# Prompt attention of a hybrid decoder step, in 12 units of a head pair instead of 24 of a head pair and a row tile

## What is computed

```python
def masked_softmax(logits, mask):
    logits = jnp.where(mask, logits.astype(jnp.float32), NEG_INF)
    m = jnp.max(logits, axis=-1, keepdims=True)
    e = jnp.where(mask, jnp.exp(logits - m), 0.0)
    return e / jnp.maximum(jnp.sum(e, axis=-1, keepdims=True), TINY)
...
    logits = (jnp.einsum('btgrd,bsgd->bgrts', qg, k).astype(jnp.float32) * ATTN_SCALE
              - alibi_slopes()[None, :, :, None, None] * dist.astype(jnp.float32))
    pr = masked_softmax(logits, mask)
    o = jnp.einsum('bgrts,bsgd->btgrd', pr.astype(v.dtype), v)
...
    logits = jnp.concatenate(
        [jnp.einsum('bthd,bshd->bhts', q, k).astype(jnp.float32) * ATTN_SCALE
         + cq_t - jnp.swapaxes(ck, 1, 2)[:, :, None, :] for k, _, _, ck in segs], axis=-1)
...
    o_a = ng[..., 0:1] * o_cmp + ng[..., 1:2] * o_sel + ng[..., 2:3] * o_win
```

## Time and profile before

| | us |
|---|---|
| median of 3 executions | 924.46 (921.75 to 925.11) |
| profiled execution | 927.73 |
| its span in the trace | 926.0 |
| PE busy | 858.2 (93%) |
| DVE busy | 513.4 (55%) |
| ACT busy | 378.6 (41%) |
| POOL busy | 161.3 (17%) |
| DMA | 191.89 MB, mean 207 GB/s |

### The profile page before, as it was taken

The page is one execution under the profiler, slowest core; times in us unless marked ns, Lnnn a source line. Parts: engine busy times, 40 slices in busy tenths (PEclk is TensorE's granted clock), DMA queues, the critical chain, the costliest instruction groups (busy, mean ns, idle before and its releaser), DMA issues. The chain is left out here.

```text
span 926.0 us, 17951 instructions
## 1 busy us (share of the span) xinstructions
PE 858.2 (93%) x7159; PEld 703.4 (76%) x7159; DVE 513.4 (55%) x941; ACT 378.6 (41%) x704; POOL 161.3 (17%) x262
## 2 busy tenths in 40 slices
PE   4999878799999999999998977999979999999997
PEld 3788768689989977655754455997678998989985
DVE  5466567533434566754467434655656565565654
ACT  4346575633334324453224322444243443444432
POOL 2000041311121022333434510000001010110100
PEclk8999989999999899999999999999979999999999
DMA  6442096155424259999999995974054544555412
GB/s 219 150 160 105 10 316 236 60 145 134 165 107 184 92 229 398 346 333 416 406 417 420 388 404 169 297 250 164 10 196 142 162 137 136 177 195 171 136 45 61
DMA packets 90640, 191.89 MB, mean 207 GB/s; under 512 B 7466, under 2 KB 68682, under 8 KB 78186
## 3 DMA queue, kind: packets, MB, share of 16 engines
q0 software_dynamic: 15408, 106.04, 29.4%
q1 hardware_dynamic: 74876, 83.91, 29.0%
q10 hardware_dynamic: 288, 0.97, 0.3%
HBM read 187.44 MB, written 7.64 MB: 211 GB/s over the span
## 5 line engine op out<-in xcount | busy, mean ns | idle before, releaser
L1627 PEld LDWEIGHTS banks<-consts_base,stream_rows 128*128 128x128 f32 x672 | 73.2, 141 | 33.9 <-issue 26.8
L1875 ACT ACTIVATE keys_turned<-banks 128x512 f32<-128x512 f32 x94 | 55.0, 597 | 98.4 <-PE banks L1627 96.2
L258 PE MATMUL banks<-tokens_turned_high,w_gates_high 128*128 128x288 f32 x288 | 86.6, 301 | 3.3 <-PEq L191 2.3
L1627 PE MATMUL banks<-consts_base,stream_rows 128*128 128x128 f32 x672 | 82.7, 276 | 7.4 <-DVE fox_probs_turned L1866 2.6
L259 PE MATMUL banks<-tokens_turned_low,w_gates_high 128*128 128x288 f32 x288 | 85.5, 297 | 0.0
L1166 PE MATMUL banks<-chunks_turned_high,cmp_w_high 64*128 64x256 f32 (+1 forms) x512 | 78.6, 300 | 5.3 <-DVE cmp_w_low L251 2.7
L260 PE MATMUL banks<-tokens_turned_high,w_gates_low 128*128 128x288 f32 x272 | 81.8, 301 | 0.0
L1166 PE MATMUL banks<-chunks_turned_low,cmp_w_high 64*128 64x256 f32 (+1 forms) x512 | 75.4, 287 | 0.0
L1166 PE MATMUL banks<-chunks_turned_high,cmp_w_low 64*128 64x256 f32 (+1 forms) x512 | 75.1, 286 | 0.0
L1856 DVE COPY keys_turned<-banks 128x512 f32<-128x512 f32 x74 | 50.2, 689 | 32.7 <-PE banks L1627 30.2
L251 DVE TENSOR_TENSOR chunks_turned_low<-banks,chunks_turned_high 128x512 fp32r<-128x512 f32 x64 | 41.1, 683 | 46.9 <-ACT chunks_turned_high L246 46.9
(11 more groups left out here) (451 smaller groups left out, 2099.1 us busy)
## 6 DMA issues: line engine op xcount, KB each, us to landing
w_up_gate<-in_w_up SPq DMA_DIRECT2D x12, 1024.0 KB, 7.3
w_up_gate<-in_w_gate SPq DMA_DIRECT2D x12, 1024.0 KB, 9.8
w_down<-in_w_down SPq DMA_DIRECT2D x12, 1024.0 KB, 4.9
w_in_slot<-in_w_in SPq DMA_DIRECT2D x7, 1424.0 KB, 6.0
w_gates<-in_w_in SPq DMA_DIRECT2D x10, 512.0 KB, 6.8
cmp_w<-in_cmp_w_k SPq DMA_DIRECT2D x4, 512.0 KB
cmp_w<-in_cmp_w_v SPq DMA_DIRECT2D x4, 512.0 KB
stream_rows<-in_state_win_k SPq DMA_DIRECT2D x8, 256.0 KB
```

The source lines that it names most:

```text
L258: nc.tensor.matmul(out, lh, rh, start=start, stop=False, **kw)
L1627: ins = nc.tensor.transpose(bank(t)[:, q * P:(q + 1) * P], src, ident)
L1875: copy = lambda a, b: nc.scalar.activation(a, b, ACT.Copy)
```

## The change

- **Units.** 12 units: (sel, r) and (win, r) for r = 0..3 in turn, then (fox, r). An NSA unit has heads r and r+4 (one of each kv head), a fox unit heads 2r and 2r+1; both row tiles are in the unit.
- **Logits.** `c.qp`, `c.fqp` keep 4 slots, head j of the pair on partitions 64j to 64j+63 without zeros; each logit matmul contracts 64 partitions, on one of the two row halves, into a PSUM bank of its own.
- **DVE** takes each of the 4 logit tiles with one `tensor_tensor_reduce` (add of a bias table, and the minimum of the negated sum): a new constant table `pbias` for NSA; for fox POOL writes mask plus running sum into a tile and over that table.
- **Scaling before turning.** Shares of all 4 row groups at once; then probabilities are multiplied by them: tile 0 by DVE, tile 1 by POOL (NSA) or DVE (fox).
- **Turned probabilities** leave PSUM by DVE (tile 0) and ACT (tile 1).
- **Values** are the stationary operand, 64 columns, turned probabilities stream (128 columns), the two heads on the two column halves. Sel and win add up in one PSUM pair. The sums come out transposed, in `c.oap`, `c.obp`; so decode's 16 transposes go, and its `branch` steps are two splits.
- **POOL's list** is rewritten: its 8 normalisations stand between the gathers, the sums over `past_logf` stay last.
- **Compressed branch.** 8 logit matmuls of 2 x 16 columns (copy `kd` of the keys by group) instead of 16 of 16; values by 4 matmuls of 256 columns instead of 2 of 512, transposed sums.

```diff
--- before.py
+++ after.py
...
-    "prompt": ("pdist", "pmask"),
+    "prompt": ("pmask",),
+    "alibi": ("pbias",),
...
-            nc.gpsimd.memset(c.qp[:, :, :], 0.0)
-            nc.gpsimd.memset(c.fqp[:, :, :], 0.0)
...
-                        dst = (c.qp[rows, g * NR:(g + 1) * NR] if q == 0 else c.fqp[rows, g:NH:2])[:, :, t * P:(t + 1) * P]
+                        dst = (c.qp if q == 0 else c.fqp)[rows, :, t * P:(t + 1) * P]
...
-    units = [(br, t, pair) for br in ("sel", "win", "fox") for t in range(QT) for pair in range(NH // 2)]
-    U = len(units)
+    units = [(br, r) for r in range(NR) for br in ("sel", "win")] + [("fox", r) for r in range(NR)]
+    U, N = len(units), 2 * NR
+    part = lambda t: slice(0, P) if t == 0 else slice(P, P + SEQ)
+    T_LAG, PV_LAG = 2, 3
...
+            def past_sums(half):
+                by_pair = lambda x: x.rearrange("p b (j h) -> p b j h", h=2)
+                by_row = lambda x: x.rearrange("p (j b h) -> p b j h", j=4, h=2)
+                lf, after = past_logf[:, half * 4:half * 4 + 4], c.logf_after[:, half]
+                pool.wait_ge(past_logf_in, 16 * DB)
...
+            def normalise(m):
+                pool.wait_ge(share_ready, m + 1)
+                x = s[m % 3][:, :, part(1)]
+                nc.gpsimd.tensor_tensor(x, x, bcast(den[m % 3][:, 1, :], 2, SEQ), ALU.mult).then_inc(normed[1], 1)
...
+            for m in range(N):
+                normalise(m)
+                if m < 2:
+                    chunks.gather(2 + m)
+                if m == 2:
+                    pool.wait_ge(logf_ready, 1)
+                    keep(*pieces[-1])
+                if 3 <= m < 7:
+                    for b in range(2):
+                        past_rows(2 * (m - 3) + b)
+                if m == 4:
+                    fox_bias_first()
+                if m >= 5:
+                    fox_bias_second(m - 5)
+            fox_bias_second(NR - 1)
...
+            def scores(m):
+                br, r = units[m]
+                if m >= 2:
+                    pe.wait_ge(neg, 4 * (m - 1))
+                for t in range(QT):
                     for j in range(2):
...
+                        rows = slice(j * HD, (j + 1) * HD)
+                        q, k = (c.fqp, c.fkT[rows, r, 0:t + 1, :]) if br == "fox" else (c.qp, c.kT[rows, 0 if br == "sel" else 1, 0:t + 1, :])
+                        ins = nc.tensor.matmul(logits(m, t, j), q[rows, r, t * P:(t + 1) * P], k, start=True, stop=br != "fox", skip_group_check=True)
+                    for j in range(2):
+                        for kt in range(t + 1 if br == "fox" else 0):
+                            ins = nc.tensor.matmul(logits(m, t, j)[:, kt * P:], nlf[:, kt, 2 * r + j:2 * r + j + 1].to_broadcast([P, P]),
+                                                   up[:, 0:(t + 1 - kt) * P], start=False, stop=(kt == t), skip_group_check=True)
+                ins.then_inc(qk, 1)
...
+            def turn(m):
+                for t in range(QT):
+                    if t and units[m][0] == "fox":
+                        pe.wait_ge(fox_normed, m - N + 1)
+                    else:
+                        pe.wait_ge(normed[t], m + 1)
+                    if m:
+                        pe.wait_ge(copied[t], m)
                     for j in range(2):
                         for kt in range(t + 1):
...
+                            at = (j * (t + 1) + kt) * P
+                            ins = nc.tensor.transpose(c.ps[3 - t][:, at:at + P], s[m % 3][:, j, (t + kt) * P:(t + kt + 1) * P], c.k("ident"))
+                    ins.then_inc(turned[t], 1)
...
+            def values(m):
+                br, r = units[m]
+                if br == "sel" and r:
+                    pe.wait_ge(nsa_out, r)
+                if br == "fox":
+                    pe.wait_ge(nsa_out, NR)
+                    if r:
+                        pe.wait_ge(fox_out, r)
+                for t in range(QT):
+                    pe.wait_ge(copied[t], m + 1)
+                    for kt in range(t + 1):
+                        for j in range(2):
+                            off = {"sel": O_SV, "win": O_WV, "fox": O_FV + r * P}[br] + j * HD
+                            ins = nc.tensor.matmul(both[j * HD:(j + 1) * HD, t, r, :], z[:, kt, off:off + HD], pT[m % 2][:, j, t + kt, :],
+                                                   start=(br != "win" and kt == 0), stop=(br != "sel" and kt == t), skip_group_check=True)
+                ins.then_inc(pv, 1)
...
+            def exponentials(m):
+                for t in range(QT):
+                    for j in range(2):
+                        act.wait_ge(neg, 4 * m + 2 * t + j + 1)
+                        x = s[m % 3][:, j, part(t)]
+                        nc.scalar.activation(x, x, ACT.Exp, scale=-1.0, bias=nm[m % 3][:, t, j:j + 1], accum_out=den[m % 3][:, t, j:j + 1]).then_inc(probs, 1)
...
+            def take_logits(m):
+                br, r = units[m]
+                dve.wait_ge(qk, m + 1)
+                if m >= 3:
+                    dve.wait_ge(turned[0], m - 2)
+                    dve.wait_ge(turned[1], m - 2)
+                if br == "fox":
+                    dve.wait_ge(fox_bias, 2 + r)
+                for t in range(QT):
+                    for j in range(2):
+                        nc.vector.tensor_tensor_reduce(s[m % 3][:, j, part(t)], logits(m, t, j), bias_of(m, t, j), -1.0, FAR, ALU.add, ALU.min,
+                                                       nm[m % 3][:, t, j:j + 1]).then_inc(neg, 1)
...
+            def normalise(m):
+                dve.wait_ge(share_ready, m + 1)
+                for t in range(QT if units[m][0] == "fox" else 1):
+                    x = s[m % 3][:, :, part(t)]
+                    nc.vector.tensor_tensor(x, x, bcast(den[m % 3][:, t, :], 2, (t + 1) * P), ALU.mult).then_inc(fox_normed if t else normed[0], 1)
...
+            for n in range(U + T_LAG):
+                if n < U:
+                    take_logits(n)
+                if n == 0:
+                    forget_logs()
+                if n == 1:
                     dve.wait_ge(cum_ready, 1)
...
+                    nc.vector.tensor_copy(cq[:, :, :], c.ps[3][:, 0:2 * NH].rearrange("p (t h) -> p t h", t=QT)).then_inc(cum_out, 1)
+                if n >= T_LAG:
+                    take_turned(n - T_LAG)
+                if 1 <= n <= U:
+                    shares(n - 1)
+                    normalise(n - 1)
+                if 4 <= n < 4 + N and n % 2 == 0:
+                    nsa_rows_out((n - 4) // 2)
...
-                    pe.wait_ge(kc_done, 1)
+                    pe.wait_ge(kd_ready, 2)
                     pe.wait_ge(vh_ready, 2)
                     for t in range(QT):
-                        for h in range(NH):
-                            ins = nc.tensor.matmul(c.ps[7][:, (t * NH + h) * PCH:(t * NH + h + 1) * PCH], c.qp[:, h, t * P:(t + 1) * P],
-                                                   c.kcT[:, ND:ND + PCH], start=True, stop=True)
+                        by_head = c.ps[7][:, t * NH * PCH:(t + 1) * NH * PCH].rearrange("p (g r c) -> p g r c", g=NG, r=NR)
+                        for r in range(NR):
+                            ins = nc.tensor.matmul(by_head[:, :, r, :], c.qp[:, r, t * P:(t + 1) * P], kd[:, :, :], start=True, stop=True)
...
-                    nc.tensor.matmul(c.ps[7][:, :] if t == 0 else bank(NSTEP - 2, 0)[:, :], pcT[:, t, :], vh[:, :], start=True, stop=True).then_inc(ppv, 1)
+                    for j in range(2):
+                        ins = nc.tensor.matmul((c.ps[7] if t == 0 else bank(NSTEP - 2, 0))[:, j * SEQ:(j + 1) * SEQ], vh[:, (2 * t + j) * P:(2 * t + j + 1) * P],
+                                               pcT[:, :, :].rearrange("p t n -> p (t n)"), start=True, stop=True)
...
-            def turn_branch(step):
-                i, t = step[3], first[step]
-                free_bank(t)
-                for j in range(4):
-                    ins = nc.tensor.transpose(bank(t)[:, j * P:(j + 1) * P], (c.oa, c.ob)[i // 2][:, i % 2, j * P:(j + 1) * P], ident)
                 ins.then_inc(turned, 1)
 
...
-                    split_high(nc, o_cols(c.branch_high, i), o_bank(t)).then_inc(branch_high, 1)
+                    split_high(nc, o_cols(c.branch_high, i), (c.oap, c.obp)[i][:, :, :]).then_inc(branch_high, 1)
...
+                if kind == "branch":
+                    dve.wait_ge(branch_high, i + 1)
+                    split_low(nc, o_cols(c.branch_low, i), (c.oap, c.obp)[i][:, :, :], o_cols(c.branch_high, i))
```

305 lines of the change are left out of this document (127 added, 178 removed).

## The result

| | before | after |
|---|---|---|
| median of 9 runs, us | 925.11 (921.32 to 929.25) | 919.19 (915.55 to 923.1) |
| ratio, 95% interval | | 0.9937 (0.9914 to 0.996) |
| profiled execution, us (span) | 927.73 (926.0) | 920.28 (918.4) |

The kernel became 5.9 us (0.6%) faster. The forecast was 11.4 faster. The profiled pair differs by 7.45 us, and the trace splits that well. I use five marks: the start of compression (SP's first load of it), its first and its last output matmuls, the start of the FFN, and the end. The prompt stage itself starts at 113.1 in both.

What follows compares the result with a forecast made beforehand. No engine filled the prompt stage (waits in each unit's round bound it), and DMA bound decode. Prompt stage -7.5, compression -4.6 and its start +0.7 gave -11.4 us, so 924.5 became 913.1 us, range 905 to 922.

Steps and rivals of the forecast that it cites:

- The walk to the end of computing: Prompt stage: unit-by-unit timing from ACT's first exponential at 117.45 us to the end of computing at 170.2.
- POOL's stretch: Prompt stage, products 3 to 7: POOL's products, gathers and bias tiles take 17.9 us against 13.6 on DVE, pacing four units.
- I leave that at 159.6: Prompt stage's end: small gathers still land at 159.6, POOL's sums last 10.9 us to 170.5, next stage starts at 171.5.
- Start of compression: First part of compression: PE stands idle longer before it, costing +0.7 us (0 to +2).
- Compression's logits: Compression: 32 narrow records become 16, 2.3 us instead of 4.66, and PE's clock stays full: -4.6 us (-2.4 if it falls).
- Decode and what follows it: Decode: 16 transposes and two PSUM rounds go, but DMA sets the pace: 0 us (-1.9 to +1).
- POOL and DVE block each other: Rival, prompt stage: DVE's product over 256 and POOL's over 512 wait for each other, +4.8 us, 917.9; chance 0.18.
- The gathers land later: Rival, prompt stage: last small gather issued 7 us later, landing follows issue, POOL ends 5 later, 918 us; chance 0.12.
- The halves don't share: Rival, PE's half-array matmuls: +1.4 us in each of six units and the tail, only compression gains, 920.5 us; chance 0.07.
- Everything better: Rival, prompt stage: rows land earlier, fox units near 3.6 us, next stage at 166 to 167, 908 us; chance 0.12.
- The clock drops in the prompt stage: Rival: PE at half clock from 131 on, next stage at 194.7, total 935.6 us; chance 0.06.
- The changes of shape: PE: switching from 64-row to 128-row tiles costs 0.09 us each, three per NSA unit, six per fox unit.

Runs made afterwards that it cites:

- the bias on ScalarE: On the kernel with early gathers, POOL's 1.91 us first-tile fox bias operation replaced by eight small ones on ScalarE in units 3 to 6: 910.92 us, ratio 0.9866.
- early gathers: Changed kernel with POOL's eight past_logf gathers issued sooner (two before the first unit, two each in units 2 to 4): 913.36 us, ratio 0.9896.
- the bias earlier on POOL: On the kernel with early gathers, POOL's first-tile fox bias operation moved from unit 4 to unit 2: 917.32 us, ratio 0.993.
- head after head: Changed kernel with a pair's matmuls reordered, all of head 0 before head 1 (its results are wrong): 918.74 us, ratio 0.9947.
- the last kernel above: Changed kernel plus early gathers, fox bias on ScalarE, both tiles' logits before the forget sums, and window-state copies behind the stores, not waited for: 907.22 us, ratio 0.9807.
- all products on DVE: On the kernel with early gathers, the second tile's probabilities in the eight gated units weighted on VectorE instead of POOL: 914.84 us, ratio 0.9896.
- the sums grouped: On the kernel with early gathers, both tiles' logits ahead of all forget sums of a fox unit: 913.18 us, ratio 0.9887; with the bias on ScalarE too, 912.12, 0.9868.
- the copies behind the stores: Changed kernel with only the two window-state copies moved last in SP's prompt-stage queue and waited for at the kernel's end: 916.8 us, ratio 0.9878.

## Why the prediction was half right

**The walk to the end of computing: 170.2 forecast, 170.7 measured with ACT's last copy (PE's end is 170.3), and that is no confirmation.** The kernels with the same units and the gathers or copies elsewhere ended PE's computing at 167.3 to 167.7, the one with the bias on ScalarE at 164.5. The forecast lacked a hole and a clock: product 5 came late behind POOL's bias tile, PE stood idle 2.6 us and then ran at half clock for 10. I had priced POOL's stretch (17.9 us from product 3 to 7; 129.3 to 150.1 measured, 20.8) and not asked what PE's clock does in it. POOL's own work was 18.0 of the 20.8; for the other 2.8 it waited, ahead of product 7, for DVE's shares, which waited for PE: POOL did not pace the whole stretch. What made up for it was ahead of that stretch, where product 3 began at 129.3 and not 131.3, and mainly DVE, which I had at 41.5 us and which was busy for 35.8. Its instructions took about what I had put in, but in a row they overlap. DVE in order of time:

```profile
124.88 0.42 DVE L997 CUSTOM_DVE_ANT_0 prompt_logits<-banks,consts_alibi 128x256 f32<-128x256 f32 x1
125.22 0.08 DVE L997 DVE_READ_ACCUMULATOR2_ANT prompt_negmax<- 128x1 f32 x1
125.22 0.42 DVE L1022 COPY prompt_probs_turned<-banks 128x256 f32<-128x256 f32 x1
125.56 0.16 DVE L1004 TENSOR_SCALAR prompt_sums<-prompt_sums 128x4 f32<-128x4 f32 x1
```

The next one starts 0.34 us after one of 0.42. I had overlap in PE's prices, taken from the starts of neighbours, and left it out of DVE's.

**The step that failed: "I leave that at 159.6", and 10.9 and 1.0 us behind it.** The floor was named and its three terms were all too small. The rows landed 1.6 us later; the sums took 11.8, since the first half (fifteen in 5.42 us and one of 0.58, against 4.93 and 0.25 before) ran beside DVE's last units; and behind POOL the next stage took 2.0 us to start, not 1.0. Together 3.5, and 171.5 + 3.5 is the 175.0 measured. The reason given, that the same bytes go through the same queues, was half of the truth: the landing depends on both. Issued 9.6 us sooner the rows landed 9.3 sooner (151.9); issued at about the same time without the copies in the stage, at least 9.8 sooner.

**Start of compression: 0.7 forecast (0 to 2.0), 2.1 measured.** The price is at the upper end of the bound: PE was idle from 170.3 to 175 and at half clock to 187. With the idle time down to 1.2 us (early gathers) the price is 0. But its size does not follow the idle time alone: with 4.2 us idle (the bias earlier on POOL) and with 8.1 (head after head) it was 0.8, and 0.8 again in the last kernel above, with 1.2.

**Compression's logits: 4.6 forecast, 4.9 measured**, 3.3 when undone by itself. The mechanism is shown, the size is known only to lie near these two.

**Decode and what follows it: 0 forecast, 0.7 measured.** The 16 transposes less moved nothing that can be told from the 588 to 591 us which the rest of the program took in the kernels here. Projection: 0 forecast, 0 measured (the prompt stage starts at 113.1 in both).

**The rivals.** *POOL and DVE block each other*: yes, though not at the price or the place given. In the pairs that the rival named, DVE's product over 256 began first and took 0.42 to 0.43 us, as in the units where it ran alone, and POOL's took 1.23 to 1.28 in five units against 1.05 in the three where it ran alone: 0.2 each, not 1.0. Where POOL began first, DVE waited to its end: 1.44 us instead of some 0.2 at 138 in the changed kernel, 2.44 with early gathers, 2.15 with all products on DVE, where PE stood idle for it. The Trainium skill (SBUF — State Buffer, Who interferes with whom) says that whichever of the two starts second fully blocks; the trace agrees where POOL was first (ends within 0.04 us of each other), and where DVE was first POOL lost 0.2 of DVE's 0.4. In the changed kernel DVE's wait cost nothing that shows (PE was busy at half clock), but the longer sums above, 0.8 us, fit the same (the one of 0.58 us ran beside DVE's product of 166.6 to 167.4). *The gathers land later*: in part; issued 5.6 us later (145.3 instead of 139.7), they landed 1.6 later, and the early gathers show that issue counts. (By the forecast's own numbers this rival would have cost 7 us, 920, and not the 5 and 918 written there.) *The halves don't share*: no, values took 0.81 us for twelve records, and 1.44 would be no sharing. *Everything better*: not in this kernel; its 166 to 167 for the start of compression was reached only with the bias on ScalarE and the sums grouped. *The clock drops in the prompt stage*: it did, for 10 us of it and not to the end, and with the hole ahead of it cost some 5 us that POOL's floor hid: from the stage's start to PE's last value matmul it took 57.2 us, 54.7 with the short dip of the early gathers, and 52.2 with the bias on ScalarE.

**The changes of shape** were priced at 0.09 each, from one row; two of them less saved 0.39, some 0.2 each. The Trainium skill (TensorEngine Tiling (Array Packing), Key Properties) names the drain. If all six of a fox unit cost as much, they are 1.2 us and not the 0.6 that I had, and as the unit took 4.66 for 4.5, my other terms were too large by some 0.4; only these two changes were measured.

**The whole.** -4.1 + 2.1 - 4.9 - 0.7 is the -7.6 of the spans; the medians say -5.9 with an interval of some 2 us to either side, which holds it.

## What to carry to other kernels

When a faster stage brings two ends together, price the other end as closely as the one you worked on: what lands when, what runs beside it, and what the barrier costs behind that engine; here three errors of 0.9 to 1.6 us ate 3.5 of the 7.5 us, and the two floors behind (late rows, late stores) came up one after another. A copy that nobody in the stage needs belongs behind that stage's loads and stores and out of its wait, not into the next stage, where it stands in front of that one's gathers. And a hole of 2 to 3 us on PE costs more than itself when the clock falls behind it, so an operation of 2 us on a helper engine, in front of what PE waits for, is better cut up and given to an engine that is idle; on POOL it also held a short instruction of DVE's for as long as it ran.

## What the runs showed of the hardware

- A stage that ended on POOL's work was followed by the next 2.0 us later in every kernel where POOL was last (172.97 to 174.97 after, 168.61 to 170.62 with the bias earlier on POOL, 169.47 to 171.48 with the copies behind the stores); behind ACT's last copy it was 0.8 (167.84 to 168.64 with early gathers; 1.0 in the kernel before), behind the last store's landing 1.0 (166.8 to 167.8 with the bias on ScalarE). The ends of POOL's instructions are rough in the trace.
- The stretch at half clock behind the same idle time of PE near 138 was 10 us long in the changed kernel, 3 with early gathers (139.5 to 142.6), 6.5 with grouped sums, and absent with head after head, where the idle time was as long in busy share (2.40 of 4 us busy in 138 to 142). What decides its length is open.
- DVE's fused addition with minimum from PSUM took 0.42 us for 256 columns and 0.29 for 128, plus 0.08 for the read of the result, near what was worked out from one instruction over 1024 columns; in a row the next starts 0.34 us after one of 0.42.
- DVE and POOL held each other up. A DVE instruction over four columns (0.15 to 0.21 us alone) lasted until POOL's running ones ended: 1.44 us in the changed kernel (to 139.42, POOL's end 139.39), 2.44 with early gathers (140.56 and 140.52), 2.15 with all products on DVE (137.27 and 137.24). DVE's additions and copies out of PSUM beside the same POOL operation kept their length (0.42 us for 256 columns at 136.95 and 137.64).
- SP stood in one issue of a small store for 15.4 us (142.5 to 157.9) with the two 2 MB copies ahead of it in its queue; with these behind the stores, all stores were issued by 143.8. An earlier stand remained there (13.7 us from 117.7, at the first store), so the copies are not the only thing that holds an issue.
